# The second score product on halves of the array, in the dilated and banded attention stages of an encoder

## What is computed

```python
def banded_attention(q, k, v, radius, sink=None):
    ...
    s = jnp.einsum('bnqhgd,bnkhd->bnhgqk', qp, kw,
                   preferred_element_type=jnp.float32) * (dh ** -0.5)
    ...
    s = jnp.where(valid[None, :, None, None], s, NEG_INF)
    m = jnp.max(s, axis=-1, keepdims=True)
    ...
    e = jnp.exp(s - m)
    den = jnp.sum(e, axis=-1, keepdims=True)
    ...
    o = jnp.einsum('bnhgqk,bnkhd->bnqhgd', (e / den).astype(v.dtype), vw)
```

## Time and profile before

| what | value |
|---|---|
| median of 3 runs | 3987.07 us (3985.03 to 3988.13) |
| span of the profiled execution, first to last instruction | 3984.4 us |
| PE matmuls busy in it | 3836.3 us, 96% |
| PE weight loads busy | 3705.1 us, 93% |
| DVE, ACT, POOL busy | 2677.0, 2108.6 and 858.6 us (67%, 53%, 22%) |
| HBM traffic | 146 GB/s over the span |

### The profile page before, as it was taken

One profiled execution on the slowest core, in us unless ns is written; L12 is line 12 of the kernel. 1 busy time (PEld: TensorE's weight loads), 2 busy tenths in 40 slices (PEclk: granted clock), 3 DMA queues, 4 the chain that ended last, 5 costly groups with the idle time before them and its releaser, 6 DMA issues. The chain is left out here.

```text
span 3984.4 us, 75741 instructions
## 1 busy us (share of the span) xinstructions
PE 3836.3 (96%) x27408; PEld 3705.1 (93%) x27408; DVE 2677.0 (67%) x5533; ACT 2108.6 (53%) x3896; POOL 858.6 (22%) x1367
## 2 busy tenths in 40 slices
PE   8999999999989799999999999999997999999998
PEld 7989989999988699999999989999886999999998
DVE  6565664676665677777777757777536777777775
ACT  6544554555542255555555556555323556555654
POOL 5132230333330011111111133323000111211122
PEclk9999999999989899999999999999998999999999
DMA  3000001122124487887788731000436777877874
GB/s 109 10 21 7 25 16 36 49 66 69 52 97 153 141 252 235 254 249 245 241 251 253 240 86 51 31 24 16 149 130 206 237 248 247 256 240 247 253 244 130
DMA packets 492028, 583.99 MB, mean 147 GB/s; under 512 B 21537, under 2 KB 447521, under 8 KB 491809
## 3 DMA queue, kind: packets, MB, share of 16 engines
q1 hardware_dynamic: 473952, 522.44, 39.9%
q0 software_dynamic: 15680, 50.34, 6.0%
q10 hardware_dynamic: 2176, 8.39, 0.5%
HBM read 514.89 MB, written 66.22 MB: 146 GB/s over the span
## 5 line engine op out<-in xcount | busy, mean ns | idle before, releaser
L1687 DVE TENSOR_TENSOR wl<-raw,wh 128x2048 fp32r<-128x2048 f32 x384 | 879.1, 2290 | 283.0 <-ACT wh L1642 269.7
L1642 ACT CAST wh<-raw 128x2048 fp32r<-128x2048 f32 x384 | 732.8, 1908 | 24.3 <-DMA raw<-in_w_gate 22.1
L1786 PE MATMUL ps_g<-xT,wh 128*128 128x384 f32 x2048 | 595.0, 357 | 0.5 <-DVE xT L1693 0.5
L1786 PE MATMUL ps_u<-xT,wh 128*128 128x384 f32 x2048 | 594.8, 357 | 0.0
L1788 PE MATMUL ps_u<-xT,wl 128*128 128x192 f32 x2048 | 477.1, 253 | 0.0
L1788 PE MATMUL ps_g<-xT,wl 128*128 128x192 f32 x2048 | 477.1, 253 | 0.0
L151 PE MATMUL psP<-ring_high,hTh 128*128 128x384 f32 (+1 forms) x1344 | 460.2, 342 | 12.5 <-DVE ring_low L810 6.2
L153 PE MATMUL psP<-ring_high,hTl 128*128 128x384 f32 (+1 forms) x1344 | 441.6, 329 | 0.0
L152 PE MATMUL psP<-ring_low,hTh 128*128 128x384 f32 (+1 forms) x1344 | 441.2, 328 | 0.0
L1059 PEld LDWEIGHTS psO<-V,pT 128*128 128x128 f32 x3456 | 417.5, 192 | 20.4 <-issue 10.2
L1059 PE MATMUL psO<-V,pT 128*128 128x64 f32 x3456 | 415.6, 272 | 5.0 <-ACT pT L746 3.0
(11 more groups left out here) (212 smaller groups left out, 8725.5 us busy)
## 6 DMA issues: line engine op xcount, KB each, us to landing
raw<-in_w_gate SPq DMA_DIRECT2D x128, 1024.0 KB, 5.2
raw<-in_w_up SPq DMA_DIRECT2D x128, 1024.0 KB, 5.1
raw<-in_w_down SPq DMA_DIRECT2D x128, 1024.0 KB, 7.2
xb<-in_x SPq DMA_DIRECT2D x72, 256.0 KB, 2.8
out_y<-yb SPq DMA_DIRECT2D x24, 512.0 KB, 2.6
h_rows<-hb SPq DMA_DIRECT2D x24, 512.0 KB, 2.9
ring_raw<-in_w_a SPq DMA_DIRECT2D x24, 384.0 KB, 3.8
xb<-in_x SPq DMA_DIRECT2D x12, 512.0 KB, 4.7
```

What stands on the lines that cost most here:

```text
L1642: act.copy(wh[:, j % SPL], raw[:, j % RAW]).then_inc(w_high, 1)
L1687: dve.tensor_tensor(wl[:, j % SPL], raw[:, j % RAW], wh[:, j % SPL].bitcast(F32), ALU.subtract)\
L1786: both = lambda **fl: pe.matmul(ps[:, f, 0:2 * CAP], wh[:, j % SPL, k, fs], xT[:, k].rearrange("p h c -> p (h c)"), **fl)
```

## The change

In the stages "a" and "c" the second product of each head is taken out of the loop and put behind the first products of both heads. It uses only the 64 rows with the high part of that head's query: rows 0 to 63 for the first head of the pair, 64 to 127 for the second. It covers all `nk * P` columns of the head at once (at most 384, so one instruction as before). The number of instructions stays the same: four weight loads and four matmuls per unit. The product of the query's low part with the keys' low part is no longer added. The dense stage is as before.

```diff
@@ -1032,7 +1032,13 @@
                         q, kv = qT[:, h, t * P:(t + 1) * P], min(h, nkv - 1)
                         ks = slice(k0 * P + w0, k0 * P + w0 + w)
                         pe.matmul(out, q, kT[:, kv, 0, ks], start=True, stop=False)
-                        ins = pe.matmul(out, q, kT[:, kv, 1, ks], start=False, stop=True)
+                        if dense:
+                            ins = pe.matmul(out, q, kT[:, kv, 1, ks], start=False, stop=True)
+                if not dense:
+                    for c, (h, t, k0, nk, mask) in enumerate(segs):
+                        rows, kv = slice(c * HD, (c + 1) * HD), min(h, nkv - 1)
+                        ins = pe.matmul(psS[:, u % 2, c * 512:c * 512 + nk * P], qT[rows, h, t * P:(t + 1) * P],
+                                        kT[rows, kv, 1, k0 * P:(k0 + nk) * P], start=False, stop=True)
                 ins.then_inc(scored, 1)
```

## The result

The changed kernel takes 4009.59 us (median of 5 runs, 4001.52 to 4042.34) where the kernel before takes 3987.07 (5 runs): by the medians it is 22.5 us or 0.6% slower; the ratio, which is not that of the two medians, is 1.0069 with a 95% interval of 1.0053 to 1.0086. The run of 4042.34 us had a mean granted clock of 0.924, the other four 0.985 to 0.988. The profiled execution is the fastest of the five, with a span of 3999.7 us, 15.3 over that of before.

What follows compares the result with a forecast made beforehand. PE was taken to bound stages a and c. Longer score units add 48 us, less 6.5 absorbed by waits: 41.5 us on the median of 3987.07 gives 4029 us, range 4006 to 4066.

Steps and rivals of the forecast that it cites:

- rival 1: Score units: halves' products and loads all side by side; 30 us less 4.5 absorbed, 4012 us; chance 0.17.
- What a change of rows costs: PE between 128 and 64 rows: 0.09 us to run empty, then a bare load, 0.11 or 0.05 for a transpose.
- rival 3: Score units: the array doesn't empty at changes of rows, so the kernel is faster, 3963 or 3975 us; chance 0.11.
- second case: Halves in score units: loads one after the other, products side by side; 48 us before absorption; the case chosen.
- first case: Halves in score units: products and loads side by side, 0.34 - s more at 384 and 256 columns; 30 us before absorption.
- What is absorbed: PE's waits behind score blocks eat added time: 4.5 us in stage a, 1.5 in stage c, 6.5 in all.
- fall to 6 us: Sign in stage a: the wait of T's first load behind score blocks would fall from 10.5 to some 6 us.
- What is late next: `scored` rises 0.2 to 0.3 us later, ahead of DVE's maximum, ACT's exponential and R; costed at nothing.
- fourth case: Score units: the array also empties between the halves, 77 us after absorption, 4064 us; chance 0.12.
- Rival 4: Score units: each product takes its step as before and boundaries cost nothing, 3987 us within 8; chance 0.04.

Runs made afterwards that it cites:

- four-head kernels: Kernel before, but stage c's four second products per tile stand together: 4007.1 us with 64 rows, 4002.8 with 128; late maximum, 64 rows, 4001.5.
- same-half kernel: Changed kernel, but both second products use rows 0 to 63: 4026.5 us, ratio 1.0104.
- half a projection between: Four-head kernel with 64 rows, but 12 projection products stand between the first pair's first products and R of the second pair: 4025.5 us, ratio 1.0102.

## Why the prediction was right, and where its size was off

**Direction and bound: right.** The time lies in the range, and on the side that was given 0.84. Stages a and c grew and the others didn't; the granted clock of these stages stayed. The forecast itself, 4029 us, was 19 us too high. The range held the time only near its lower end, 4006, which had been set by rival 1, and rival 1 had a chance of 0.17: the number is right by the width of the range and not by the case that was chosen.

**What a change of rows costs: right.** Predicted were 0.26, 0.21 and 0.15 from the second high product to the halves' load; by the start times in the trace the medians are 0.267, 0.207 and 0.202. At 128 columns it is 0.05 more, which I left out: there the second product's load takes 0.11 and begins only 0.06 ahead of the start on record (1056.34 and 1056.40 in the kernel before), so 0.05 of it is still to come. On the way out the medians are 0.37, 0.31 and 0.25, and 0.26, 0.20 and 0.15 without the halves' load of 0.11, as predicted. A figure read off eight transposes in another stage held for products in reduced format; the doubt in rival 3 was not borne out.

**The step that failed** is the choice of the second case for the halves ("loads one after the other, products side by side"). Both loads run at once, as the result's timeline shows, and rival 1 holds: 0.34 - s. From start to start, the transpose behind it included, a unit costs 0.168, 0.193 and 0.158 more by width, 80 x 0.168 + 56 x 0.193 + 32 x 0.158 = 29.3 us, where the first case had 30 and I took 48. So stage a grew by 8.0 us and not by 15, stage c by 13.8 and not by 27. The argument for single file was that no two loads stood at once in the trace; but the loads there fill all or most of the 128 rows or, in the eight transposes, the same 64, so that the trace could not show two on different halves. That absence should have carried less weight than it was given, and the page's rule more: the Trainium skill ("TensorE: Matmul & The Clock Gate", Part 3) has matmuls of different row groups start about 4 ns apart. The trace agrees: here the two products start 3 ns apart.

**What is absorbed: right, a little low.** 29.3 less 21.8 by stages is 7.5 us, 4 of it in stage a and 3.5 in stage c; for this case 4.5 was given. The first loads of T behind a score block wait 11.8 us over 28 times in stage a now (waits of the weight loads between 696 and 1176 us), after 10.5 over 15 times:

```profile
PEld psT L1017 <- issue: 11.8, 28, 1.2
```

The fall to 6 us that I named as a sign did not show. 13 of the 28 last 0.19 each, 2.4 us together, the gap that any unit of 384 columns has now; the other 15 make 9.4 us and hold this gap as well.

**What is late next: right in its price, wrong in its size.** I had `scored` 0.2 to 0.3 us later and cost it at nothing. It is 0.02 to 0.08 us later, so that this run hardly tries the cover. The four-head kernels show what a later one does: the first pair's halves end at 2463.54, 2.16 us behind the start of its block in place of 0.95, DVE stands before `scored`, and PE pays at the changes of pass.

**Rivals.** The fourth case (empty between the halves) is excluded, for two different halves by the result and for twice the same half by that experiment. The Trainium skill ("TensorEngine Tiling (Array Packing)", Key Properties) has a change of mode drain the engine, "not just tile". The trace agrees: each change of rows costs 0.09 us and a bare load, the change of half 0.003 us. Rival 3 (the array doesn't empty) is excluded by the loads of the halves, which start 0.27, 0.21 and 0.20 us behind the second high product and not beside it. Rival 4, "it does not do what it says", is excluded by the same rows and by the same-half kernel, 17 us slower.

## What to carry to other kernels

Halves of the array run truly side by side, loads and products, but going from 128 rows to 64 and back costs about 0.34 us per visit with float32 data at the full clock (0.09 to empty, 0.11 for a bare load, 0.09 to empty again, 0.05 for a bare transpose load), while a pair saves one step of 0.11 to 0.175: a visit must save two steps of 384 columns to break even, and no kernel here saved more. Read the price of a mode change where the kernel already makes one, however far from the change; and where a trace can't show two things at once because they never could be, take both ends as open. Before work is held back to share such a price, look at what it covered and at whose queue stands behind its semaphore. And compare two profiles tile by tile, with the granted clock beside them: a few us at half clock can look like a price of the change.

## What the runs showed that I had not expected

- Two weight loads for different halves take the time of one (0.18 for both records, 0.11 until the products run); on the same half they go in single file (0.29).
- The array takes 0.20 us from the start of a transpose, and 0.26 from that of a product of 384 columns, until a load for the other number of rows starts, the same on the way in and, behind the halves' own load, on the way out: some 0.09 us more than the stream's step.
- Holding the first pair's second products back, with no work added on any engine, made stage c 14.6 us longer at 128 rows.
- The same waits of PE, 1.6 us at a change of pass, were followed by a granted clock of 0.50 in one profile and of 1.00 in another; with half a projection between, waits of 2.1 us were followed by 6.8, 6.8 and 13.7 us at 0.50.
